# Splitting the modulation of norms two to four between VectorE and ScalarE in a two-layer SSM, attention and MoE network

## The reference

```python
def rmsnorm(x, w):
    xf = x.astype(jnp.float32)
    y = xf * lax.rsqrt(jnp.mean(xf * xf, axis=-1, keepdims=True) + EPS)
    return y.astype(x.dtype) * w

def modulate(x, shift, scale):
    return x * (1 + scale) + shift
...
for l in range(DEPTH):
    a_l = modulate(rmsnorm(h, norm1_w[l]), sh1, sc1)
    a_c = modulate(rmsnorm(hc, norm1_w[l]), csh1, csc1)
    ...
    m_l = modulate(rmsnorm(h, norm2_w[l]), sh2, sc2)
    h = h + g2 * grouped_moe(m_l, ...)
```

## Time and profile before

| | |
|---|---|
| median of three executions | 1531.84 us (1531.24 to 1535.51) |
| profiled execution, its time and span | 1540.6 us; the profile gives its span only, no time of its own beside it |
| TensorE matmul, busy | 1427.9 us (93%) |
| VectorE, busy | 538.1 us (35%) |
| ScalarE, busy | 389.7 us (25%) |
| mean granted TensorE clock | 0.967 of full speed |
| modulations at L808 | 56 instructions, 28.2 us busy |

### The profile page before, as it was taken

How to read it: one execution, slowest core, us unless ns; L and a number is a source line. 1 busy time by engine, 2 the same in 40 slices (tenths; PEclk the granted TensorE clock), 3 DMA queues, 4 the chain that set the end, 5 groups by cost and what they waited for, 6 DMA issues and landing times.

```text
span 1540.6 us, 29201 instructions
## 1 busy us (share of the span) xinstructions
PE 1427.9 (93%) x12493; PEld 826.6 (54%) x12493; DVE 538.1 (35%) x977; ACT 389.7 (25%) x958; POOL 187.4 (12%) x213
## 2 busy tenths in 40 slices
PE   6999898999988999989999999998999999999876
PEld 3534444554544444464666566645856776565432
DVE  2445666455443221144121221124254441221112
ACT  2312333433434210040121221103053301221111
POOL 0000134223252200000011111000000001111100
PEclk9799999999999999999999999998999999999987
DMA  9365344334341452142999999992330349999993
GB/s 354 113 211 188 113 137 137 112 135 137 112 158 32 109 137 82 70 179 79 367 351 372 382 386 385 354 359 89 124 110 1 127 177 391 394 393 398 401 402 128
DMA packets 131493, 334.48 MB, mean 217 GB/s; under 512 B 13283, under 2 KB 63259, under 8 KB 125211
## 3 DMA queue, kind: packets, MB, share of 16 engines
q1 hardware_dynamic: 118763, 307.56, 55.0%
q0 software_dynamic: 6208, 12.60, 2.4%
q10 hardware_dynamic: 6384, 12.36, 2.3%
HBM read 325.79 MB, written 14.81 MB: 221 GB/s over the span
## 4 chain that ended last, share of the span: by engine, by line
PE 75%; SPq 10%; DMA 6%; DVE 4%; ACT 3%; issue 2%; DVEq 0%; ACTq 0%; POOLq 0%
PE ps L1500 12%; PE ps L1182 11%; SPq L557 7%; PE ps L1199 7%; PE ps L1396 7%; PE ps L1539 6%; PE ps L1450 5%; PE ps L1125 3%; SPq L559 2%; PE ps L1287 2%; PE ps L1800 2%; PE ps L1564 2%; PE ps L1712 2%; PE ps L1274 2%; DMA ring<-in_moe_w_down 1%
## 5 line engine op out<-in xcount | busy, mean ns | idle before, releaser
L1182 PE MATMUL ps<-aT,ring 128*128 128x512 f32 x384 | 174.7, 604 | 0.0
L1500 PE MATMUL ps<-ring,ssb 128*32 128x256 f32 x2256 | 139.4, 391 | 9.9 <-DMA ring<-in_moe_w_up 9.2
L1500 PE MATMUL ps<-tmp,ssb 128*32 128x256 f32 x1984 | 116.8, 382 | 6.1 <-DMA tmp<-in_moe_w_up 6.1
L2218 DVE COPY big<-ps 32x256 f32<-32x256 f32 x162 | 68.6, 423 | 144.0 <-PE ps L1539 142.3
L1500 PEld LDWEIGHTS ps<-ring,ssb 128*32 128x32 f32 x2256 | 86.9, 112 | 55.8 <-DMA ring<-in_moe_w_up 15.2
L1182 PEld LDWEIGHTS ps<-aT,ring 128*128 128x128 f32 x384 | 71.3, 193 | 83.0 <-issue 82.9
L1199 PE MATMUL ps<-aT,ring 128*128 128x512 f32 x256 | 114.2, 595 | 0.0
L2209 DVE TENSOR_TENSOR ssb<-ssb,ps 128x128 f32<-128x128 f32 (+1 forms) x56 | 19.1, 347 | 263.0 <-ACT ssb L976 261.7
L1396 PE MATMUL ps<-big,ring 128*128 128x512 f32 x256 | 110.2, 592 | 0.0
L1539 PE MATMUL ps<-ring,ssb 128*32 128x256 f32 x1648 | 96.9, 388 | 2.3 <-DMA ring<-in_moe_w_down 1.7
L883 ACT ACTIVATE ssb<-ps,ncum 128x128 f32<-128x128 f32 x256 | 73.1, 371 | 96.5 <-PE ps L1262 95.7
(11 more groups left out here) (389 smaller groups left out, 1846.0 us busy)
## 6 DMA issues: line engine op xcount, KB each, us to landing
ring<-in_ada_w SPq DMA_DIRECT2D x44, 1024.0 KB
ring<-in_moe_w_down SPq DMA_DIRECT2D x40, 1024.0 KB
ring<-in_moe_w_gate SPq DMA_DIRECT2D x56, 512.0 KB
ring<-in_moe_w_up SPq DMA_DIRECT2D x56, 512.0 KB
tmp<-in_moe_w_gate SPq DMA_DIRECT2D x48, 512.0 KB
tmp<-in_moe_w_up SPq DMA_DIRECT2D x48, 512.0 KB
ring<-in_ssd_in_w SPq DMA_DIRECT2D x20, 1024.0 KB
tmp<-in_moe_w_down SPq DMA_DIRECT2D x16, 1024.0 KB
```

The lines of the kernel that those rows point to most:

```text
L1182: ins = pe.matmul(ps[:, bank, :], slot(u)[:, k, (i % 2) * P:(i % 2 + 1) * P], aT[:, k, :], start=(k == 0), stop=(k == KD - 1))
L1500: ins = pe.matmul(tiled_gu[32 * c:32 * c + 32, 2 * h + i, :].rearrange("p (r n) -> p r n", r=2), XgT[l][:, k * C + 32 * g:k * C + 32 * g + ...
L2218: ins = dve.tensor_copy(Y[s % 2][32 * g:32 * g + 32, 256 * c:256 * c + 256], tiled_y[32 * c:32 * c + 32, 2 * h + i, :])
```

## The change

In norms 1 to 3 VectorE makes the product of an odd tile, then that of the even tile before it, and then modulates the odd tile itself by a `tensor_scalar` with two operands per partition. ScalarE modulates the even tiles only. `s_a` then counts the even tiles, `s_nx` counts products of even tiles and finished odd tiles in turn, and TensorE waits for one or the other by the parity of the tile (`modulated`). GpSimd waits for both counts. Norm 0 is as before.

```diff
+def acts_to(i):
+    return KD * min(i, 1) + KD // 2 * sum(NORM_PARTS[1:i])
...
             def moe_pool(l):
-                pool.wait_ge(s_a, parts_to(2 * l + 2))
+                pool.wait_ge(s_a, acts_to(2 * l + 2))
+                pool.wait_ge(s_nx, parts_to(2 * l + 2))
...
                 for h in range(NORM_PARTS[i]):
-                    for k in range(KD):
+                    for k in range(0, KD, 2 if i else 1):
                         act.wait_ge(s_nx, parts_to(i) + KD * h + k + 1)
...
+            def modulated(i, h, k):
+
+                if i == 0:
+                    pe.wait_ge(s_a, k + 1)
+                elif k % 2:
+                    pe.wait_ge(s_nx, parts_to(i) + KD * h + k + 1)
+                else:
+                    pe.wait_ge(s_a, acts_to(i) + KD // 2 * h + k // 2 + 1)
...
                                 if q == 0 and r == 0:
-                                    pe.wait_ge(s_a, parts_to(i) + KD * h + k + 1)
+                                    modulated(i, h, k)
...
                 for k in range(KD):
-                    pe.wait_ge(s_a, parts_to(2) + KD * h + k + 1)
+                    modulated(2, h, k)
...
             def norm(i, n, between={}):
                 dve.wait_ge(s_rs, rstd_to(i) + 1)
+                l, m = divmod(i, 2)
...
-                    for k in range(KD):
+                    for k in range(0 if i else KD):
                         if k in between:
                             between[k](0)
                         dve.tensor_tensor(aT[:, k, part], hT[:, k, part], rstd[:, part], ALU.mult).then_inc(s_nx, 1)
+                    for k in range(0, KD if i else 0, 2):
+                        dve.tensor_tensor(aT[:, k + 1, part], hT[:, k + 1, part], rstd[:, part], ALU.mult).then_inc(s_v, 1)
+                        chain[0] += 1
+                        dve.tensor_tensor(aT[:, k, part], hT[:, k, part], rstd[:, part], ALU.mult).then_inc(s_nx, 1)
+                        dve.wait_ge(s_v, chain[0])
+                        if k == 0:
+                            dve.wait_ge(s_mod, AMOD_N[l, m])
+                        for q in range(per * h // S, per * (h + 1) // S):
+                            ins = dve.tensor_scalar(aT[:, k + 1, q * S:(q + 1) * S], aT[:, k + 1, q * S:(q + 1) * S],
+                                                    amod[:, l, m, k + 1, q:q + 1], mod[:, l, 24 * m + k + 1, q:q + 1],
+                                                    ALU.mult, ALU.add)
+                        ins.then_inc(s_nx, 1)
```

## The result

The changed kernel is slower than the kernel before by 0.29%: ratio 1.0029, 95% interval 1.0017 to 1.004. Its median is 1537.34 us over 12 executions (1535.49 to 1541.14), that of the kernel before, taken beside it, 1533.32 us over 12 (1530.65 to 1536.47). On 1533.3 us the ratio is +4.4 us, interval +2.6 to +6.1. I had forecast +1.8 us and "same" as the likeliest case. The ratio lies just inside the bound of 0.3%, but its interval holds neither 1 nor my 1.8 us. The +4.4 us lie above the +2.7 that my terms gave at the most; only the outer range, which rival (a) had widened to 1537.4 us, reaches so far.

The account below looks back on a forecast made before the run. TensorE was taken as the bound, at half clock at norms 1 and 2, with VectorE's queue on the chain at norm 3. Terms 0.25 + 0.25 + 1.28 = +1.8 us on 1531.84 gave 1533.6 us, range 1531.0 to 1537.4.

Parts of the forecast that it names:

- my terms: Delays at norms 1, 2 and 3: 0.25, 0.25 and 1.28 us, with bounds +1.2 to +2.7 us in all.
- rival (a): Norm 3: longer TensorE idle before L1414 makes the clock fall, losing 3.4 us, 1537.0 us in all; chance 0.19.
- What bounds the kernel: Chain through all three norms; TensorE at half clock, not ScalarE, bounds norms 1 and 2; VectorE's products and copies follow at norm 3.
- Norms 1 and 2: First matmul starts 0.34 us later at each; cost taken as 0.25 us each, between 0.17 and 0.34.
- Norm 3, VectorE's queue: Longer VectorE work ahead of the copies delays L1414 in full: 400 ns per `tensor_scalar`, 0.99 us a pair, +1.28 us.
- Norm 3, TensorE behind the gap: Idle before L1414 grows from 1.10 to about 2.3 us; clock assumed to stay full, so no cost in the sum.
- The sum: Norms 1, 2 and 3 together: 0.25 + 0.25 + 1.28 = +1.8 us, giving 1533.6 us.
- (b): Norm 3's delay is hidden because the experts' weight stream sets the end; leaves 0.5 us, 1532.3; chance 0.10.
- (c): The split speeds the norms by cutting TensorE's wait for ScalarE; at best -0.5 us, 1531.3; chance 0.06.

Follow-up runs that it names:

- g2: Kernel before with two of six norm 3 copies on ScalarE and eight unused matmuls ahead of norms 1 and 2 each; ratio 0.9974 (0.9955 to 0.9994).
- g1: Kernel before, unaltered, run again for a second trace; one execution, span 1530.8 us.
- f1: The whole change run again, unaltered, against the kernel before; ratio 1.0018 (0.9998 to 1.0039).
- e1: Kernel before with only norm 3 split, norms 1 and 2 unchanged; ratio to before 1.002 (1.0002 to 1.0038).
- e4: Kernel before, no split, with three linked unused VectorE products between norm 3 and its copies; ratio to before 1.0008 (0.9991 to 1.0025).
- f4: The change with the even tile's product ahead of the odd tile's; one execution, norm 3 root to router's product 10.49 us, then 27.67 to list of rows.
- e2: Kernel before with only norms 1 and 2 split, norm 3 unchanged; ratio to before 1.0008 (0.9989 to 1.0027).
- g3: The change with eight unused matmuls ahead of norms 1 and 2 each and four in the norm 3 gap; ratio to before 0.9994 (0.9978 to 1.001).
- e3: The change with four unused matmuls filling TensorE's gap before layer 1's router products; ratio to before 1.0037 (1.002 to 1.0053).
- f2: The change with four unused matmuls in the gap before layer 1's router products, run again; ratio to before 1.0024 (1.0007 to 1.0042).
- f3: Kernel before, no split, with two of the six copies behind norm 3 moved to ScalarE; ratio to before 0.9982 (0.9962 to 1.0002).

## Why the prediction was wrong

**What bounds the kernel: right.** TensorE at half clock was the bound at norms 1 and 2; with the clock held in g2 the stages shrank by 1.7 to 2.8 us.

**Norms 1 and 2: right in size.** Between traces with the same stays of the clock the split costs, at norm 1, 17.41 against 17.25 us (the change and g1), 0.16; at norm 2, 19.68 against 19.35, 0.33. I had 0.25 each, between 0.17 and 0.34, and the traces show both of these cases: at norm 1 the clock fell 2.9 us behind the root in both kernels, so it came back as early with the later matmul; at norm 2 the whole stay of 3.4 us lay behind the first matmul in both, and the later first matmul cost its full 0.33.

**Norm 3, VectorE's queue: right.** 1.00 us a pair for 0.99, 407 ns for 400, and 10.00 - 8.72 = +1.28 us on the stage for +1.28. My estimate from the Trainium skill, page "VectorE: DVE Perf Modes", section "Side-by-side: where the cycles go for N=2048 bf16", was 298 ns for the `tensor_scalar` and 0.87 us for the stage. The trace does not agree: it has 407 ns and 1.28 us.

**Norm 3, TensorE behind the gap: the step that failed.** I had left the clock out of the sum and kept it as rival (a), at a chance of 0.19. Its condition was stated rightly: TensorE's idle time before L1414 grew from 1.10 to 2.15 us (2.3 worked out), and a granted clock of 0.50 followed. At this place it came every time: in all five traces with that gap unfilled and 2.15 us or longer (the change, f1, e1, e4, f4) the clock fell, in all eight with the gap at 1.11 us or less it did not. The row that should have swayed me stood in my own text: 2.2 us idle and a clock of 0.50 right behind the earlier trace rows. I had discounted it because the work ahead of it was different. The price was mis-sized as well: I took 3.4 us, half of a stay as long as that of the earlier trace rows; here the clock stayed down for 3.4 us, and the stage lost 1.48 (f4) to 1.65.

A gap of this length does not bring the fall by itself, though. Behind the gap of the earlier trace rows, ahead of the first expert of layer 1, the clock stayed at 1.00 in g1 (2.30 us idle) and in e2 (2.10 us). And every kernel has a gap of 2.18 us in the scan of layer 0, which the change does not touch: right behind it the clock fell in six of the thirteen traces and not in the other seven. Timeline and stretch in g1, then in e1:

```profile
186.62 0.64 PE L1244 MATMUL ps<-cparts,c 128*64 128x128 bf16 x8 [2.18 <-DVE tmp L1973]
...
186.60:190.00 3.40, 3.38 (x36) 3.38 (x38) 3.26 (x5) 0.60 (x1) 0.00 (x0) 0.50 0.00 0
...
185.85 0.41 PE L1259 MATMUL ps<-cparts,c 128*64 128x128 bf16 x8 [2.18 <-DVE tmp L2001]
...
185.90:190.00 4.10, 4.10 (x55) 3.56 (x56) 3.96 (x6) 0.60 (x1) 1.83 (x2) 1.00 0.00 0
```

So the fall was a matter of chances, which these rows put well above my 0.19. What decides besides the length of the gap, and whether five of five at norm 3 is partly luck, these runs do not show.

**The sum.** With that term it is 0.16 + 0.33 + 1.28 + 1.53 = 3.3 us, and the ends of the traces of the change and g1 lie 1534.2 - 1530.8 = 3.4 us apart. That this fits so well is partly luck: from the root of norm 1 to the list of rows of layer 1, where all four terms lie, the two differ by 3.1 us; the rest is scatter of other stages, 0.2 us less ahead of norm 1 and 0.5 more behind the list. The interval of the ratio is 2.6 to 6.1. So the terms found are enough, though times of whole executions cannot exclude another one to three microseconds.

**The rivals.** (b), the delay hidden by the stream of weights, is spoken against by the traces: from the first expert of layer 1 to the sum of the pairs it takes 262.2 us in the change and 262.3 in g1, so the whole of that stage moved with its start. The first expert itself started 8.7 us behind the list in the change, where the clock fell again ahead of it, and 7.8 us in g1, where it did not; how much of that reaches the end is not shown. (c), a gain by the split, fell in g3 at norm 1: with the clock held, where ScalarE's pace does bound the first part, the split was slower still, because a pair on VectorE takes as long as two modulations on ScalarE, 1.00 against 0.99 us.

## What to carry to other kernels

Before work is moved to an engine off the critical path, look at what else stands in its queue: here six copies that TensorE waited for came behind the modulated tiles, and all that VectorE took up, 1.28 us, came out at the router's products. Price a longer wait of TensorE by the wait and by what the clock does behind it; a row of the same trace with a gap as long is better evidence than a hope that the circumstances differ, and several traces say how often the fall comes. Where a stage is worth one microsecond and executions scatter by ten, compare the same stage over several traces, and take the time of whole executions only as a check.

## What the runs showed of the hardware

The scatter of executions has much to do with the clock as well. The stretch from the last products of the shared expert of layer 0 to the root of norm 2 is the same work in all kernels; it took 44.7 to 44.8 us in three traces where the clock stayed at 1.00 (the change, g1, e3; a fourth, g3, has 43.6), 45.8 to 46.7 where it stood at 0.50 once for 3.4 us (e1, e2, e4, f2, f3, g2), and 47.8 to 48.0 where it did so for 6.8 us (the first trace of before, f1, f4). The stretches of f1 there:

```profile
1040.00:1046.40 6.40, 4.41 (x40) 4.21 (x38) 1.58 (x4) 0.00 (x0) 0.00 (x0) 1.00 1.09 349
1046.40:1053.00 6.60, 5.87 (x7) 2.52 (x8) 5.50 (x15) 5.46 (x9) 0.00 (x0) 0.50 0.39 126
```

Where the stay begins counts too. At norm 1 all kernels but g2 and g3 have one of 6.8 us. In e1 and e2 it began 0.3 us behind the root and the stage up to the router's products took 16.0 and 16.1 us; in the others it began 2.8 to 3.1 us behind the root, and the stage took 17.2 to 17.4.

A `tensor_scalar` of 128x256 f32 with two operands per partition takes 407 ns, with constants 295 ns. A `tensor_scalar` that has to wait for the product right in front of it starts 0.45 us behind that product's start (f4); where it waits for the one before, it starts 0.34 us behind the product in front (the change).
